# A diffusion step on one core: first projections in quarters of the features, expert 0's rows by one-hot products, output projection on four banks, last scaling on ScalarE and GpSimd

## The reference

```python
sh1, sc1, g1, sh2, sc2, g2 = split(silu(cond) @ w_ada + b_ada, 6)    # cond: c for latent, c_ctx for context
h = ln_plain(x) * (1 + sc1) + sh1
q_a, k_a, v_a, q_g, k_g, v_g, r_g, lr, mg = split(h @ w_in)
...                                             # attention, and gated linear attention (GLA) in both directions
merged = gates[:, :, 0] * (attn @ w_br_attn) + gates[:, :, 1] * (gla @ w_br_gla)
x = ln_affine(ALPHA * x + g1 * (merged @ w_out), ln1_g, ln1_b)
h2 = ln_plain(x) * (1 + sc2) + sh2
# top-2 of the 8 experts of the best of 4 groups
for e in range(32):
    hid = silu(t @ exp_w_gate[e]) * (t @ exp_w_up[e])
    y = y + comb[:, e:e + 1] * (hid @ exp_w_down[e])
x = ln_affine(ALPHA * x + g2 * y, ln2_g, ln2_b)
```

## Time and profile before

| | us |
|---|---|
| median of 3 runs | 675.63 (674.58 to 676.66) |
| the profiled execution's own time | 672.36 |
| its span | 670.6 |
| PE busy in it | 621.0 (93%) |
| VectorE | 265.9 (40%) |
| GpSimd | 115.6 (17%) |
| ScalarE | 106.6 (16%) |
| chain that ended last: PE, DMA, VectorE | 60%, 22%, 8% |

### The profile page before, as it was taken

How to read it: one execution, slowest core, us unless ns; L and a number is a source line. 1 busy time by engine, 2 the same in 40 slices (tenths; PEclk the granted TensorE clock), 3 DMA queues, 4 the chain that set the end, 5 groups by cost and what they waited for, 6 DMA issues and landing times.

```text
span 670.6 us, 8592 instructions
## 1 busy us (share of the span) xinstructions
PE 621.0 (93%) x3403; PEld 344.4 (51%) x3403; DVE 265.9 (40%) x593; ACT 106.6 (16%) x222; POOL 115.6 (17%) x114
## 2 busy tenths in 40 slices
PE   6999999999999999999999998999999887788994
PEld 3553355546455556555544464665566544444541
DVE  4322533145445544302224865334333232222347
ACT  2001553110032222330000021111111111111000
POOL 4000000010300000000001323334334222221102
PEclk9999999999999999999999999999999999988998
DMA  9998737344131130409995097899999999999862
GB/s 336 376 332 289 251 127 251 126 158 157 24 127 58 69 126 1 126 0 317 372 402 223 38 359 296 333 420 416 413 414 417 413 417 414 415 416 419 352 241 94
DMA packets 56200, 176.65 MB, mean 263 GB/s; under 512 B 10644, under 2 KB 12724, under 8 KB 44512
## 3 DMA queue, kind: packets, MB, share of 16 engines
q1 hardware_dynamic: 39264, 143.34, 55.4%
q10 hardware_dynamic: 11152, 24.47, 10.4%
q0 software_dynamic: 5744, 8.28, 3.5%
HBM read 174.58 MB, written 11.96 MB: 278 GB/s over the span
## 4 chain that ended last, share of the span: by engine, by line
PE 60%; DMA 22%; DVE 8%; issue 2%; POOL 2%; ACT 2%; SPq 2%; ACTq 0%; DVEq 0%; POOLq 0%
PE bank L1592 13%; PE bank L1865 11%; DMA X<-exp_w_up 8%; PE bank L1581 7%; PE bank L1766 6%; PE bank L1874 5%; DMA Y<-exp_w_up 4%; PE bank L1545 3%; DMA Y<-ln_b 3%; DMA X<-w_ada 2%; PE bank L1505 2%; DMA Y<-w_ada 2%; POOL rstd L689 2%; PE bank L1839 2%; PE bank L1733 1%
## 5 line engine op out<-in xcount | busy, mean ns | idle before, releaser
L1865 PE MATMUL bank<-X,Y 128*64 128x256 f32 x672 | 82.0, 395 | 11.8 <-DMA X<-exp_w_up 10.8
L1592 PE MATMUL bank<-Y,W 128*128 128x384 f32 x256 | 86.6, 492 | 0.0
L1865 PEld LDWEIGHTS bank<-X,Y 128*64 128x64 f32 x672 | 50.7, 137 | 48.0 <-DMA X<-exp_w_up 18.0
L689 POOL TENSOR_TENSOR rstd<-ss,cst 128x1 f32<-128x1 f32 (+3 forms) x21 | 22.6, 1075 | 295.7 <-DVE ss L822 295.7
L1592 PEld LDWEIGHTS bank<-Y,W 128*128 128x128 f32 x256 | 47.4, 190 | 36.0 <-issue 5.6
L1581 PE MATMUL bank<-W,Y 128*128 128x512 f32 x144 | 64.0, 597 | 0.0
L732 POOL DMA_INDIRECT Y<-h_rows,gidx x32 | 41.4, 1293 | 92.9 <-PE bank L1839 88.4
L1192 DVE COPY abias<-bank 128x128 f32<-128x128 f32 x32 | 9.3, 292 | 117.1 <-PE bank L1898 117.1
L1865 PE MATMUL bank<-W,Y 128*64 128x256 f32 (+1 forms) x320 | 37.2, 346 | 7.5 <-DMA W<-exp_w_up 3.9
L737 POOL DMA_INDIRECT pair_rows<-PTr,sidx x32 | 32.9, 1029 | 61.2 <-DVE PTr L1206 60.6
L1779 PE MATMUL bank<-X,Y 128*128 128x512 f32 x96 | 41.7, 594 | 1.3 <-issue 1.0
(11 more groups left out here) (232 smaller groups left out, 723.2 us busy)
## 6 DMA issues: line engine op xcount, KB each, us to landing
X<-exp_w_gate SPq DMA_DIRECT2D x22, 1024.0 KB, 22.1
X<-exp_w_up SPq DMA_DIRECT2D x22, 1024.0 KB, 26.1
X<-exp_w_down SPq DMA_DIRECT2D x22, 1024.0 KB, 26.6
Y<-w_ada ACTq DMA_DIRECT2D x16, 1024.0 KB, 8.2
W<-w_in SPq DMA_DIRECT2D x7, 2048.0 KB, 9.0
W<-exp_w_gate SPq DMA_DIRECT2D x10, 1024.0 KB, 22.1
W<-exp_w_up SPq DMA_DIRECT2D x5, 1024.0 KB, 26.7
W<-exp_w_down SPq DMA_DIRECT2D x5, 1024.0 KB, 29.7
```

The lines of the kernel that those rows point to most:

```text
L689: nc.gpsimd.tensor_tensor(rstd[:, 0:n], ss[:, 0:n], const("mhalf", 0, n), ALU.pow)\
L1592: ins = mm(bank[:, 0:TOKENS], w[:, k, c * P:(c + 1) * P], hT[:, :, k, :], start=k == 0, stop=k == KT - 1)
L1865: ins = mm(bank[hh * 64:hh * 64 + 64, a:b], x_[:, c, h * 64:h * 64 + 64], rhs(hh), start=k == 0 and a == 0, stop=k == KT - 1, skip_group_c ...
```

## The change

- **Quarters.** The four adaLN products of shift and scale become four of 2 x 256 columns (`shift_scale`): each gives two feature blocks' shift and scale. kvl and gqk are formed in four parts of two blocks; in each of the first three rounds stand three kvl parts, three gqk parts, and the next `shift_scale` and `columns`. SP asks for weights in this order, in runs of 256 columns of w_ada, and for all constants but the identity and a selection behind the second quarter. The first norms' statistics are taken ahead of SiLU of the condition, and GpSimd has its -1/2 from a memset. The ring's first halves are asked for behind the last `shift_scale`.
- **Output projection** on banks 0, 1, 4, 5; the last tile in products of 512, 256 and 256 columns. ln1's gain and shift have a home of their own (PTr) and are asked for ahead of the branch products' end; gate2's rows are asked for behind h2.
- **Expert 0's rows**: VectorE compares slot numbers with the ranks (`first_slots`, 128x64 for each tile), PE multiplies them with h2, ScalarE copies the result to where the gather put it. The gather of expert 0 goes; SP's load of slot 5's up weights waits for these products.
- **Last experts**: PE forms gate/up 31 ahead of hidden and down 30; SP asks for down 30 behind up 31, and for down 31 in two halves. Residual products change places, add_rows(0, 0) moves behind down 31.
- **Last norm**: for the two latent tiles ScalarE multiplies by rstd and GpSimd adds the shift; VectorE keeps the context tile.

```diff
@@ constants and rounds
-FILL_NORM, FILL_ROUTER, FILL_RANK, FILL_GATHER = 4, 5, 2, 4
+FILL_NORM, FILL_ROUTER, FILL_RANK = 4, 6, 1
...
+WO_COLS = {(n, i): slice(n * HALF, (n + 1) * HALF) for i in range(TILES) for n in range(2)}
+WO_COLS[1, LAST_TILE] = slice(HALF, HALF + HALF // 2)
+WO_COLS[2, LAST_TILE] = slice(HALF + HALF // 2, 2 * HALF)
...
+        last = Banks((0, 1, 4, 5), banks, full, read, last_jobs(), uses)
+        expert0 = Banks((1,), banks, full, read, [("rows",)], uses)
@@ SP
+            for g in range(QUARTERS):
+                load_shift_scale(g)
+                load_quarter(g)
+                if g == 1:
+                    sp.dma_start(cst[:, early_consts:], T["consts"][:, early_consts:NCONST]).then_inc(S["consts_in"], 16)
+            small_loads()
...
-            side.wait_full(sp, "hT", TILES - 1, 1)
+            expert0.wait_full(sp, "rows")
             load_part(sp, "exp_w_up", 1, PARTED, PARTED, ew_in[PARTED])
@@ GpSimd
-            for n in range(NSLOT):
+            for n in range(1, NSLOT):
                 gather_rows(n)
...
-            for i in range(TILES):
-                power(1)
+            pool.wait_ge(S["ln2_in"], 32)
+            power(1, 0)
+            for i in range(TILES - 1):
+                power(1, i + 1)
+                pool.wait_ge(S["out_scaled"], i + 1)
+                nc.gpsimd.tensor_tensor(fin(i, 0), fin(i, 0), ln2(1), ALU.add).then_inc(S["out_ready"], 1)
@@ VectorE
+            for i in range(TILES):
+                ins = V.tensor_scalar(first_slots[:, i, :], const("iota_rows", 0, SLOT_ROWS), bank[:, i * NE:i * NE + 1],
+                                      both[:, i, 0:1], ALU.is_equal, ALU.mult)
+            ins.then_inc(S["onehot_ready"], FIRST_SLOTS)
@@ ScalarE
-            main.wait_full(act, "ada", 3)
+            main.wait_full(act, "shift_scale", QUARTERS - 1)
             for h in range(3):
                 ada_half(h)
...
+            for i in range(TILES - 1):
+                act.wait_ge(S["pow_done"], OTHER_POWERS + i + 1)
+                act.wait_ge(S["scaled"], i + 1)
+                A_(fin(i, 0), fin(i, 0), ACT.Copy, scale=rstd[:, i:i + 1]).then_inc(S["out_scaled"], 1)
@@ PE
+            def shift_scale(g):
+
+                pe.wait_ge(shift_scale_in[g], 32)
+                bank = main.claim(pe, "shift_scale", g)
+                for s in range(2):
+                    w = early[2 * s + g // 2][:, g % 2]
+                    for k in range(KT):
+                        j = k % 4
+                        ins = mm(bank[32 * j:32 * j + 32, s * QD:(s + 1) * QD], csil[:, k, :], w[:, k, :], start=k < 4,
+                                 stop=k >= 4, skip_group_check=True)
+                main.filled(ins, "shift_scale", g)
...
+            shift_scale(0)
             x_transposes(2)
+            columns(0)
+            keep_busy(FILL_QUARTER)
+            for g in range(QUARTERS - 1):
+                for i in range(TILES):
+                    project_quarter("kvl", i, g)
+                project_quarter("gqk", 0, g)
+                shift_scale(g + 1)
+                project_quarter("gqk", 1, g)
+                columns(g + 1)
+                project_quarter("gqk", 2, g)
...
+            pe.wait_ge(S["onehot_ready"], FIRST_SLOTS)
+            bank = expert0.claim(pe, "rows")
+            for i in range(TILES):
+                for h in range(2):
+                    ins = mm(bank[h * SLOT_ROWS:(h + 1) * SLOT_ROWS, :], first_slots[:, i, :],
+                             xr(i)[:, h * HALF:(h + 1) * HALF], start=i == 0, stop=i == TILES - 1, skip_group_check=True)
+            expert0.filled(ins, "rows")
```

459 lines of the change are left out of this document (230 added, 229 removed).

## The result

The changed kernel took 680.4 us in the median of 4 runs (680.32 to 681.35), beside 675.1 of the kernel before on the same chip: a ratio of 1.0071, with a 95% interval of 1.0048 to 1.0094. (The ratios given are not quotients of the medians beside them and differ from those by up to 0.08%.) That is slower, by more than twice the 0.3% that the prediction took as its bound, and 0.9 us above its range. The start is missed alike in both profiled executions, so this closer number is no merit of the sum.

A forecast was written before the change was run, and what follows sets the result against it. PE's chain was taken to bind outside the weight stream's plateau, where DMA hides its work. Terms +4.1 - 1.8 - 2.9 + 0.5 = -0.1 us on the median of 675.63 gave 675.5 us, range 669.5 to 679.5.

The forecast's parts named there:

- the start's +4.1: Start in feature quarters: 2.5 us for the later fourth w_ada half plus 1.6 for the clock; bounds -3 and +7.
- First kvl product at 19.5: Start: fewer bytes asked for ahead, so the first kvl product comes at 19.5 us, 6.0 us earlier.
- kvl complete at 56.0: Start: three rounds and the last kvl quarters take 36.5 us, so kvl is complete 2.5 us later than before.
- The fourth half 2.5 us later, at 67.8: Start: the fourth w_ada half arrives 2.5 us later than 65.27, with z(0) behind it on PE; bounds 1.5 and 4.5.
- The clock +1.6, once: Start: PE idles over 4 us at the fourth half, so products behind run slower, +1.6; a second fall taken as 0.
- second rival: Slower: z(0) 4.5 us later for the queued half and the clock falls twice, +3.2; total +3.5, 679.1 us; chance 0.24.
- Output projection, -1.8: Output projection: four banks, ln1 early and a narrower last chunk save 1.8 us; bounds -2.5 and -1.0.
- Expert 0's rows, -2.9: Ahead of gate/up 0: replacing the gather by compares and products saves 2.9 us; bounds -3.5 and -1.5.
- expert 1's rows: Expert 1's gather, 1.4 us later against its indices, lands about when wanted, hidden by gate/up 0 (3.85 us).
- Tail, +0.5: Last norm: GpSimd's later add delays tile 1's output, partly hidden by ScalarE's half, +0.5; bounds -0.5 and +2.0.
- the sum goes onto the median: Baseline: the -0.1 us sum is added to the median of 675.63, not the profiled 672.36, giving 675.5.
- the plateau: Weight stream from 436 to 620 us at 413 to 420 GB/s: PE is not the bound, changes there costed at nothing.

The follow-up runs named there:

- the twelve later ones: The unchanged change run again twelve times against the kernel before: 678.85 us, ratio 1.0020.
- start filled: The changed kernel with three more filling products at the start, around x's tile transposes: 677.62 us, ratio 1.0020.
- the filled kernels: The changed kernel with filling products either at the start (677.62 us) or ahead of the second half of adaLN product 5 (676.30 us).
- ring halves early: The changed kernel with two of the three first w_ada ring halves asked for behind shift/scale product 2, some 10 us earlier: 675.08 us, ratio 0.9980.
- adaLN 5 behind z(1): The changed kernel with adaLN product 5 moved behind gqk's last quarter, z(0), z(1) and lr(2): 671.32 us, ratio 0.9933.
- the late ln2: The changed kernel with ln2's two loads asked for by ScalarE at expert 29, no longer behind h2: 680.81 us, ratio 1.0066.
- filling the wait: The changed kernel with four filling products ahead of the second half of adaLN product 5: 676.30 us, ratio 0.9997.
- the start-as-before kernel: The changed kernel with its start undone (constants in one request, adaLN matrices and feature halves again), all else as changed: 670.36 us, ratio 0.9914.
- the last kernel above: The changed kernel with its start mended and tail on VectorE, plus gate2 and ln2 asked for later: 670.79 us, ratio 0.9928.
- the start as before with the tail on VectorE: The changed kernel with the start of the kernel before and the tail's scalings on VectorE again: 669.66 us, ratio 0.9900.
- the rows' product alone: The kernel before with nothing changed but expert 0's rows formed by one-hot products: 674.43 us, ratio 0.9962.
- the second profile of before: The kernel before, unchanged, run and profiled again: 676.61 us, ratio 1.0005; profile span 674.8 us.

## Why the prediction was wrong, step by step

**The step that failed is the start's +4.1.** It cost 8.15 us at vg 0 in the first profile and, with the slow vg product counted, 9.8 in the second; undoing it gave 10.6 us against the first four runs (1.0071 less 0.9914, of 676) and 7.2 against the twelve later ones (1.0020). z(0) came 7.2 us later (73.47 and not 66.27), where 4 was forecast. Its own parts:
- *First kvl product at 19.5.* Right where the clock holds (19.17 to 19.89 in five executions, three of them with the start filled), wrong in the change's own two: 22.16 and 20.55. The step took PE to be free "behind the second tile's transposes" and did not ask how long it idles ahead of them: 2.17 us. By the earlier trace rows, with a fall behind 2.02 us, that idle was a candidate. In 5 executions with this start, at 2.16 or 2.17 us, the clock fell; in 2, at 1.88 and 2.04 us, it held. It costs up to 2.9 us in an execution; filling it brought nothing in the median.
- *kvl complete at 56.0.* It is 55.4 and 55.5 in the filled kernels and 58.35 in the change: right, and carried along by the missed fall.
- *The fourth half 2.5 us later, at 67.8.* With the start filled it is used at 68.33: right in size and in cause, the queue (ring halves early: 2.6 us back) with z(0) behind it on PE. The largest lever was that order and not the transfer: adaLN 5 behind z(1) took off 6 to 9 us (0.9933 against 1.0020 and 1.0071; 1.0066 for the late ln2, which has the unmended start and ran on the same chip).
- *The clock +1.6, once.* Too small. The rows of products that follow the wait are not one group: product 5's half, z(0) and the gqk quarter run cold (0.86, 0.95 and 1.25 us more in the change), and in three executions of this start the vg product as well (2.4 to 2.7 us more). What is lost is shown by filling the wait: 1.8 us, of some 3 us of colder products, since z(1)'s chain hides a part.
- The prediction's second rival, start +7.7, was the case that came, with 679.1. It put both falls behind the wait; one of them was in fact at x's second tile.

**Output projection, -1.8: right in its stretch.** From the first output product to the last tile's aggregate 43.33 us and not 44.99, -1.7. The wait for ln_b is gone, PE has no stall, and VectorE begins the last chunk 0.5 us behind PE's end. **Expert 0's rows, -2.9: right alone** (-2.94 to the refill request, -2.5 us of time), and from the first output product to gate/up 0's end the change has 72.64 us, 4.8 less than before, where 4.7 was forecast. The compares took 1.00 us and not 0.65.

**Costed at nothing, and not nothing: expert 1's rows.** The prediction had this gather land about when it is wanted. It is in the chain (421.00, 4.34 us) and lands 0.3 us behind gate/up 0's end at 425.06; PE goes on 1.37 us behind that end, and gate/up 1 begins 3.3 us behind it, where that was 1.9. gate2, moved because its first use is late, is not shown to be the reason: its four loads have all landed by 420.2, ahead of the gather's request, and the start-as-before kernel with the same requests has no such wait. With ln2 asked for at expert 29 there is none either; with gate2 next to this gather (the last kernel above) it is 1.63 us and not 1.21. So what travels beside a gather moves it by a microsecond or so, and which transfer did it in the change was not separated. Expert 0's gather is off PE's path.

**Tail, +0.5: the mechanism right, the engine that pays wrong.** GpSimd's last add runs behind the last power, and SP sends tile 1's 512 KB at 672.52, next to the halves of tile 2. The add was not stretched (2.34 us, 2.35 without company). VectorE was: the first of its two scalings took 2.13 us and ended 0.54 us behind the add, the second 0.74. So it stood through most of the add. From the start of PE's last group to the end of the span it is 12.1 us, and 9.9 and 10.8 in the two profiles of before: +1.3 to +2.2, partly given back by PE, which needs 1.3 us less from the last up weights on. The Trainium skill (SBUF — State Buffer, SBUF: two separate sides) states that of a VectorE instruction with two SBUF inputs and a GpSimd instruction that reads SBUF the one that starts first keeps the ports they share for its whole instruction and the other stands still. The trace agrees to 0.2 us: the scaling ended 0.54 us behind the add, and one takes 0.75 without company. The prediction had looked for the loss on GpSimd; GpSimd started first, at 670.15.

**The baseline.** With "the sum goes onto the median" terms read from an unusually fast execution, without a clock fall at the start, were added to the median of slower ones. The rest of the change is worth 4.2 us by the forecast's own terms and 5.7 by the time with the start undone; in the profiles the difference from the first output product to the span's end is 0.9 against the first of before and 3.8 against the second. What the median of before holds beyond those 1.3 to 2.0 us at its start was not settled, nor why the stretch behind the first refill request is 249.6 to 250.9 us in three executions (both of before, and the start as before with the tail on VectorE) and 251.6 to 255.1 in the others, 254.0 with the rows' product alone among them. (In the second profile of before the request itself comes 1.4 us behind gate/up 0's end.) In the change this stretch is 3.6 us longer than in the first profile of before, where the forecast has 0.5: the tail takes 2.2, PE's last products give back 1.3, and the other 2.7 lie in the plateau, which the prediction put at nothing; their cause is open.

## What to carry to other kernels

Splitting the first loads so that PE starts earlier moves the wait, and what stands behind the next wait in program order pays for it: look for work that does not need the late data and issue it first. Before an idle of PE is costed at its length, add what the products behind it cost at the lower clock, all of them down to the next wait that hides it; with this start the clock fell behind some 2 us of idle in 5 executions of 7, though filling that idle showed no gain in the median. When a load is moved because its deadline allows it, ask what it will travel beside. And check a milepost against the median before a gain is booked on it: one first refill request came 6.2 us earlier and the ratio did not move.

## What was not expected of the hardware

The clock's fall is not a function of one idle's length alone: gate/up products behind 2.02 to 2.05 us of idle took 5.44 us in some executions and 3.85 in others (591.67, start filled, against the earlier trace rows), and in the second profile of before it fell behind waits of 0.69 and 1.07 us. The profile that the prediction rests on has a row that held too, 57.6 us ahead of the one that fell in the earlier trace rows (PE's timeline of before), and in the change a product held behind 2.35 us (622.06, 3.85 us):
```profile
532.41 3.84 PE L1865 MATMUL bank<-X,Y 128*64 128x256 f32 x32 [2.09 <-DMA X<-exp_w_up]
```
The twelve later runs of the change lie 6.8 us apart (675.57 to 682.37); the shorter ones have the higher granted clock (above), and a cold vg product alone costs 2.7 us; which falls each run had is not known, since one of them was profiled. The Trainium skill (TensorE: Matmul & The Clock Gate, What's actually happening) says that the number of products at the lower clock differs between runs of one kernel; vg 0's 7.03 and 9.77 us in the two profiles of the change agree. In runs of 1 KB w_ada and the loads beside it moved at 351 GB/s from 15 to 20 us, beside 382 in the kernel before; whether the shorter runs or the different set of transfers cost anything there was not tried alone.
